# Second weights of experts 6 to 29 in one transfer each, in a one-core decoder layer with 32 experts

## The reference, cut to what matters

```python
hn = rms_norm(x, norm_ffn_g)
logits = hn @ router_w + router_b            # 256 x 32; the best 4 per token, softmax over them
gu = xb @ w_gu[e] + b_gu[e]                  # w_gu[e]: 1024 x 2048, float32, 8 MB
x_glu = minimum(gu[:, :1024], 7.0)
x_lin = clip(gu[:, 1024:], -7.0, 7.0)
act = x_glu * sigmoid(1.702 * x_glu) * (x_lin + 1.0)
y = act @ w_down[e] + b_down[e]              # w_down[e]: 1024 x 1024, float32, 4 MB
x = x + sum over the 4 experts of gate * y
out = rms_norm(x, norm_final_g)
```

## Time and profile before

| | before |
|---|---|
| runs of the kernel, median (lowest to highest) | 1183.41 us (1183.18 to 1184.78), 3 runs |
| the profiled execution, its own time | 1185.09 us |
| span of that execution in the trace | 1183.3 us |
| busy share of PE / DVE / ACT / POOL | 95% / 29% / 18% / 1% |
| data moved, mean rate over the span | 449.67 MB, 380 GB/s |
| mean granted clock of PE | 0.994 of full |

### The profile page before, as it was taken

How to read it: one execution, slowest core, us unless ns; L and a number is a source line. 1 busy time by engine, 2 the same in 40 slices (tenths; PEclk the granted TensorE clock), 3 DMA queues, 4 the chain that set the end, 5 groups by cost and what they waited for, 6 DMA issues and landing times.

```text
span 1183.3 us, 16067 instructions
## 1 busy us (share of the span) xinstructions
PE 1123.7 (95%) x6921; PEld 549.1 (46%) x6921; DVE 348.5 (29%) x668; ACT 217.9 (18%) x351; POOL 8.6 (1%) x20
## 2 busy tenths in 40 slices
PE   8999999999999999999999999999998999999996
PEld 8999878884333333333333333333333333333332
DVE  6747985556111111111111111111111211111112
ACT  5557666443000000000000000000000000000002
POOL 1000000001000000000000000000000000000000
PEclk9999999999999999999999999999999999999999
DMA  9645655799999999999999999999999999999995
GB/s 271 263 165 168 216 216 206 269 385 377 412 428 430 432 425 430 430 429 431 431 429 430 431 431 430 430 431 431 431 430 429 417 431 431 430 430 431 429 428 222
DMA packets 47993, 449.67 MB, mean 380 GB/s; under 512 B 6352, under 2 KB 9488, under 8 KB 30224
## 3 DMA queue, kind: packets, MB, share of 16 engines
q1 hardware_dynamic: 47392, 447.70, 90.8%
q10 hardware_dynamic: 560, 1.36, 0.5%
HBM read 447.48 MB, written 1.05 MB: 379 GB/s over the span
## 4 chain that ended last, share of the span: by engine, by line
PE 52%; DMA 42%; DVE 4%; ACT 2%; issue 1%; SPq 0%; ACTq 0%; DVEq 0%
DMA dn<-in_w_down 32%; PE ps L790 16%; PE ps L824 13%; DMA gu<-in_w_gu 7%; PE ps L520 6%; PE ps L526 3%; DMA dn_last<-in_w_down 2%; PE ps L499 2%; PE ps L503 2%; PE ps L500 2%; PE ps L767 2%; PE ps L730 2%; PE ps L708 1%; PE ps L808 1%; DVE w_lo L1245 0%
## 5 line engine op out<-in xcount | busy, mean ns | idle before, releaser
L790 PE MATMUL ps<-gu,xg 128*64 128x512 f32 x2048 | 450.8, 598 | 6.3 <-DMA gu<-in_w_gu 6.3
L790 PEld LDWEIGHTS ps<-gu,xg 128*64 128x64 f32 x2048 | 144.7, 138 | 308.7 <-issue 297.6
L824 PE MATMUL ps<-dn,actT 128*64 128x512 f32 x992 | 223.2, 597 | 36.7 <-DMA dn<-in_w_down 36.5
L1567 DVE TENSOR_SCALAR g<-ps 128x512 f32<-128x512 f32 x32 | 22.1, 692 | 660.4 <-PE ps L790 660.4
L824 PEld LDWEIGHTS ps<-dn,actT 128*64 128x64 f32 x992 | 67.1, 137 | 183.3 <-issue 116.0
L767 PE MATMUL ps<-y_sb,wT 64*128 64x512 f32 x248 | 67.6, 633 | 0.0
L1142 ACT ACTIVATE wT<-ps 128x256 f32<-128x256 f32 x22 | 8.5, 384 | 313.1 <-PE ps L802 313.1
L499 PE MATMUL ps<-x_hi,w_hi 128*128 128x256 f32 x256 | 65.0, 290 | 1.1 <-DVE x_lo L1252 1.1
L500 PE MATMUL ps<-x_lo,w_hi 128*128 128x256 f32 x256 | 63.6, 285 | 0.0
L1245 DVE TENSOR_TENSOR w_lo_rows<-land,w_hi_rows 128x1024 fp32r<-128x1024 f32 x48 | 56.5, 1218 | 19.7 <-ACT w_hi_rows L967 19.6
L1148 ACT ACTIVATE y_sb<-ps 128x512 f32<-128x512 f32 x22 | 13.1, 597 | 265.0 <-PE ps L824 265.0
(11 more groups left out here) (259 smaller groups left out, 875.8 us busy)
## 6 DMA issues: line engine op xcount, KB each, us to landing
gu<-in_w_gu SPq DMA_DIRECT2D x54, 4096.0 KB, 27.1
dn<-in_w_down SPq DMA_DIRECT2D x62, 2048.0 KB, 23.4
gu<-in_w_gu SPq DMA_DIRECT2D x20, 2048.0 KB, 13.1
land<-in_w_in SPq DMA_DIRECT2D x13, 2048.0 KB, 8.0
land<-in_w_proj_rnn SPq DMA_DIRECT2D x2, 2048.0 KB, 7.7
land<-in_w_proj_attn SPq DMA_DIRECT2D x2, 2048.0 KB, 9.3
land<-in_w_out SPq DMA_DIRECT2D x2, 2048.0 KB, 7.8
dn_last<-in_w_down SPq DMA_DIRECT2D x1, 2048.0 KB, 27.0
```

The source lines that it names most:

```text
L790: last = mm(ps[64 * h:64 * h + 64, 4 + c, :], xg[:, k * SLOTS:(k + 1) * SLOTS], gu[par][m // 2][:, m % 2 * 2 + r, c * D + h * HALF:c * D + ...
L824: last = mm(ps[64 * h:64 * h + 64, bank, :], src[:, j, half * SLOTS:(half + 1) * SLOTS], room[:, j, h * HALF:(h + 1) * HALF], start=half = ...
```

## The change

D(6) to D(29) are each loaded by one transfer of 4 MB into `dn_whole`, which lies where `dn[0]` and `dn[1]` lie; partition p holds eight adjacent rows (32 KB) instead of four rows of each half (16 KB each). SP waits for both halves of down(e-1) before it issues D(e), where it waited for each half. PE waits once, for the whole D(e), before down(e) (`down_whole`), with the same 32 products as before; it still raises `dn_used` twice. So that the activations match the new order of rows, DVE reads the PSUM bank with a step of eight columns instead of four, and `turn_act` makes 16 products of 64 x 64 outputs with one half of the identity each in the place of the four transposes. Experts 0 to 5, 30 and 31 keep two halves, and so do the further passes (taken only when an expert has more than 64 tokens, line 255).

```diff
+DN_WHOLE = 8
...
+        dn_whole = at("dn_whole", 64, [P, DN_WHOLE, D])
...
-        def by_rows(t):
-            return t.rearrange("q (j p) -> q j p", j=DN_RUN)
-
-        def by_columns(t):
-            return t.rearrange("q (p j) -> q j p", j=DN_RUN)
+        def by_rows(t, run=DN_RUN):
+            return t.rearrange("q (j p) -> q j p", j=run)
+
+        def by_columns(t, run=DN_RUN):
+            return t.rearrange("q (p j) -> q j p", j=run)
...
+            def load_whole(row, used):
+
+                sp.wait_ge(dn_used, used)
+                sp.dma_start(dn_whole[:, :, :], w_dn_rows[ds(row, D), :].rearrange("(p j) n -> p j n", p=P)).then_inc(
+                    whole_landed, 16)
...
             load_gu(RING * D + D, 1, lambda m: sp.wait_ge(gu_used, 4 * RING + (m + 1 - 4)))
-            load_dn(RING * D, lambda h: sp.wait_ge(dn_used, 2 * RING + (h + 1 - 2)))
+            load_whole(RING * D, 2 * RING)
             with sp.Fori(RING // 2 + 1, N_E // 2 - 1, 1) as i:
                 load_gu(i * (2 * D), 0, lambda m: sp.wait_ge(gu_used, 4 * (2 * i) + (m + 1 - 8)))
-                load_dn(i * (2 * D) - D, lambda h: sp.wait_ge(dn_used, 4 * i + (h + 1 - 4)))
+                load_whole(i * (2 * D) - D, 4 * i - 2)
                 load_gu(i * (2 * D) + D, 1, lambda m: sp.wait_ge(gu_used, 4 * (2 * i) + (m + 1 - 4)))
-                load_dn(i * (2 * D), lambda h: sp.wait_ge(dn_used, 4 * i + (h + 1 - 2)))
+                load_whole(i * (2 * D), 4 * i)
             E = N_E - 2
             load_gu(E * D, 0, lambda m: sp.wait_ge(gu_used, 4 * E + (m + 1 - 8)))
-            load_dn((E - 1) * D, lambda h: sp.wait_ge(dn_used, 2 * E + (h + 1 - 4)))
+            load_whole((E - 1) * D, 2 * E - 2)
             for m in range(4):
                 sp.wait_ge(gu_used, 4 * E + (m + 1 - 4))
...
+            def turn_act(E, par, whole=False):
                 pe.wait_ge(act_ready, E + (par + 1))
+                if whole:
+                    for j in range(DN_WHOLE):
+                        for h in range(2):
+                            rows = slice(64 * h, 64 * h + 64)
+                            last = mm(ps[rows, 7, j * SLOTS:(j + 1) * SLOTS], act_s[:, j * SLOTS:(j + 1) * SLOTS],
+                                      ident[:, rows], start=True, stop=True)
+                    last.then_inc(actT_filled, 1)
+                    return
                 for j in range(4):
                     last = nc.tensor.transpose(ps[:, 7, j * P:(j + 1) * P], act_s[:, j * P:(j + 1) * P], ident[:, :])
                 last.then_inc(actT_filled, 1)
...
-                pe.wait_ge(dn_landed[half], 16 * e + 16 * (5 - RING))
+
+                pe.wait_ge(dn_landed[half], 16 * e - 16 * (N_E - 2 - 5))
...
+            def down_whole(e, bank=6):
+
+                pe.wait_ge(whole_landed, 16 * e - 16 * (RING - 1))
+                for j in range(DN_WHOLE):
+                    for h in range(2):
+                        last = mm(ps[64 * h:64 * h + 64, bank, :], actT[:, j // 2, j % 2 * SLOTS:(j % 2 + 1) * SLOTS],
+                                  dn_whole[:, j, h * HALF:(h + 1) * HALF], start=j == 0, stop=j == DN_WHOLE - 1)
+                    if j % DN_RUN == DN_RUN - 1:
+                        last.then_inc(dn_used, 1)
...
-                turn_act(E, par)
+                turn_act(E, par, second is None)
...
-                for half in range(2):
-
-                    room = second(E + (par - at_once), half)
-                    down(half, room).then_inc(dn_used, 1)
+                if second:
+                    for half in range(2):
+
+                        room = second(E + (par - at_once), half)
+                        down(half, room).then_inc(dn_used, 1)
+                else:
+                    down_whole(E + par)
...
                 if not first:
-                    for half in range(2):
-                        down(half, wait_second(E + (par - 1), half)).then_inc(dn_used, 1)
+                    down_whole(E + (par - 1))
...
-                turn_act(E, par)
+                turn_act(E, par, whole)
...
-            step(N_E - 2, 0)
+            step(N_E - 2, 0, whole=False)
...
-                        expert(p * N_E + 2 * i, p * PER_PASS + 2 * i - 1, par, at_once=True)
+                        expert(p * N_E + 2 * i, p * PER_PASS + 2 * i - 1, par, at_once=True, second=wait_second)
...
-                V.tensor_scalar(by_rows(g1[:, :]), by_columns(ps[:, 4, :]), LIMIT, None, ALU.min).then_inc(glu_ready, 1)
-                V.tensor_scalar(by_rows(l1[:, :]), by_columns(ps[:, 5, :]), LIMIT, -LIMIT, ALU.min, ALU.max).then_inc(gu_read, 1)
+                V.tensor_scalar(by_rows(g1[:, :], run), by_columns(ps[:, 4, :], run), LIMIT, None, ALU.min).then_inc(glu_ready, 1)
+                V.tensor_scalar(by_rows(l1[:, :], run), by_columns(ps[:, 5, :], run), LIMIT, -LIMIT, ALU.min, ALU.max).then_inc(gu_read, 1)
...
-            with dve.Fori(1, STEPS // 2, 1) as i:
+            with dve.Fori(1, RING // 2, 1) as i:
                 for par in range(2):
                     expert(2 * i, 2 * i, 2 * i, par)
+            with dve.Fori(RING // 2, STEPS // 2, 1) as i:
+                for par in range(2):
+                    expert(2 * i, 2 * i, 2 * i, par, run=DN_WHOLE)
             with dve.Fori(STEPS // 2, N_E // 2 - 1, 1) as i:
                 for par in range(2):
-                    expert(2 * i, 2 * i, 2 * i, par, 7)
+                    expert(2 * i, 2 * i, 2 * i, par, 7, DN_WHOLE)
```

More of the change, by code:

```diff
@@ L200, in program @@
         early_landed = [[sem(f"early_landed{p}_{m}") for m in range(4)] for p in range(2)]
-        dn_landed = [sem(f"dn_landed{r}") for r in range(3)]
+        dn_landed, whole_landed = [sem(f"dn_landed{r}") for r in range(3)], sem("whole_landed")
         (vec_landed, rope_landed, wx_landed, wa_landed, b4_landed, rw_landed, rbb_landed,
@@ L803, in turn_weights @@
                 last.then_inc(wT_filled, 1)
-            def turn_act(E, par):
+            def turn_act(E, par, whole=False):
                 pe.wait_ge(act_ready, E + (par + 1))
+                if whole:
[6 more added lines that the diff above has]
+                    return
                 for j in range(4):
@@ L827, in down, with expert @@
                 return last
-            def expert(E, X, par, meanwhile=None, first=False, at_once=False, early=0, second=wait_second):
+            def down_whole(e, bank=6):
[6 more added lines that the diff above has]
+                        last.then_inc(dn_used, 1)
+            def expert(E, X, par, meanwhile=None, first=False, at_once=False, early=0, second=None):
                 up(E, X, par, first, early, at_once)
@@ L860, in expert, with step @@
                     combine(par, 1)
-            def step(E, par, first=False):
+            def step(E, par, first=False, whole=True):
                 pe.wait_ge(wT_ready, E + par)
@@ L1563, in _, with activation @@
             dve.wait_ge(parts_ready, TT)
-            def activation(E, par):
+            def activation(E, par, run=DN_RUN):
                 dve.wait_ge(gu_used, 4 * E + 4 * (par + 1))
-                V.tensor_scalar(by_rows(g1[:, :]), by_columns(ps[:, 4, :]), LIMIT, None, ALU.min).then_inc(glu_ready, 1)
-                V.tensor_scalar(by_rows(l1[:, :]), by_columns(ps[:, 5, :]), LIMIT, -LIMIT, ALU.min, ALU.max).then_inc(gu_read, 1)
+                V.tensor_scalar(by_rows(g1[:, :], run), by_columns(ps[:, 4, :], run), LIMIT, None, ALU.min).then_inc(glu_ready, 1)
+                V.tensor_scalar(by_rows(l1[:, :], run), by_columns(ps[:, 5, :], run), LIMIT, -LIMIT, ALU.min, ALU.max).then_inc(gu_read, 1)
                 dve.wait_ge(gu_read, E + (par + 2))
@@ L1578, in keep_actT, with expert @@
                 V.tensor_copy(to[:, :, :], ps[:, 7, :].rearrange("p (j s) -> p j s", j=4)).then_inc(actT_ready, 1)
-            def expert(E, X, e, par, bank=6):
+            def expert(E, X, e, par, bank=6, run=DN_RUN):
                 build(e + (par + 1), 1 - par)
-                activation(E, par)
+                activation(E, par, run)
                 dve.wait_ge(gathered, X + (par + 2))
```

## The result

| | before | changed |
|---|---|---|
| runs of the kernel, median (lowest to highest) | 1183.42 us (1183.18 to 1184.78), 5 runs | 1190.72 us (1188.29 to 1191.22), 5 runs |
| ratio, 95% interval | | 1.0048 (1.0037 to 1.006) |
| profiled execution, its own time / span | 1185.09 / 1183.3 us | 1190.79 / 1189.1 us |

The change costs about 0.5%, some 5.7 us, in the direction and at the place that were forecast, and 1.6 us more than the 4.1 of the sum. The ratio of 1.0048 gives 1189.1 on the 1183.41 from which the sum started. The medians alone lie 7.3 us apart, and the median itself, 1190.72, lies just above the range; with five runs that scatter over 2.9 us I go by the ratio.

What follows compares the result with a forecast made beforehand. The transfer stream bounds the kernel, fed with nothing in hand where the order changes. A hole at D(23) costs 4.6 us, larger pieces return 0.5; 4.1 added to 1183.41 gives 1187.5 us, range 1185.0 to 1190.3.

Steps and rivals of the forecast that it cites:

- the sum: Whole kernel: stream 4.6 us late at D(23), 0.5 given back by six more experts; 4.1 added to 1183.41.
- What bounds the kernel: Whole kernel: the transfer stream bounds; the queue has nothing in hand only where the order changes, at expert 22.
- The pieces: Loads of D: 32 KB pieces instead of 16 KB save 0.08 us per expert, bounds 0 and 0.16.
- Rival C: Loads of D: one 4 MB transfer is cheaper than G's rows say; at 0.5 us per expert 1178.3; chance 0.06.
- The one wait in form `expert`: Before down(e): two 1.2 us waits become one of about 2.4, PE work 3.44 us later; no price there.
- The turn: Sixteen products replacing four transposes: price by columns 0, taken as 0.25 us, hidden in the wait in form `expert`.
- DVE's step of eight: DVE reading PSUM with step eight instead of four: taken as 0, far bound 1.4 us.
- The sum to D(23): From D(21)'s landing: down(21) starts 893.9, D(23) is issued 945.8 and lands 958.4 on an idle queue.
- rival A: At down(21): the clock falls in the merged wait, D(23) issued 1.7 us later, 1189.2 us; chance 0.16.
- rival B: At D(23)'s issue: hole covered if PE is 6.3 us earlier than in the sum; 1181.6 us; chance 0.10.

Runs made afterwards that it cites:

- e4: Kernel before with one wait moved: D(23)'s first half waits for both halves of down(22); 1187.36 us, ratio 1.0022 to the kernel before.
- e3: Changed kernel, still one transfer and one wait, but old row order (16 KB runs), four transposes, DVE step of four; 1192.9 us, ratio 1.0076.
- e7: Changed kernel, loops cut open, D(20) and D(21) in two transfers with two waits each, D(22) and D(23) whole; 1185.1 us, ratio 1.001.
- e6: Changed kernel, loops cut open, with the turn by four transposes again for all experts; 1189.3 us, ratio 1.0054 to the kernel before.
- the control: Changed kernel with its loops over the experts cut open at experts 20 to 25, nothing else changed; 1189.63 us, ratio 1.0051.
- e2: Changed kernel with D(6) to D(29) in two transfers and two waits on each side again; new rows, turn, DVE step kept; 1184.79 us, ratio 1.0007.
- e8: Changed kernel with D(20) to D(23) exactly as in the kernel before, the other twenty whole; 1183.64 us, ratio 0.9998.
- e9: The kernel of e8 measured once more to narrow its interval; 1183.98 us, ratio 0.9996 to the kernel before.
- e1: Changed kernel with eight more bf16 products on PE in each wait for D(e) of experts 6 to 21; 1188.54 us, ratio 1.0042.

## Why the prediction was right, point by point

- **What bounds the kernel.** Right: the stream of transfers, fed with nothing in hand only where form `expert` gives way to `step`. The one hole is there and nowhere else, and e4 shows that an issue 3.6 us later there is 2.6 us of time by the ratio, 3.5 by the medians.
- **The pieces.** Right, 0.08 us per expert: a period of 29.13 us against 29.21 in e3 and 29.22 before. Rival C (one transfer costs less than the rows of G say) fell with it, and with it the fixed cost of about 2 us that the Trainium skill names ("DMA: Bandwidth & Descriptors", section on the anatomy of one DMA) as a gain to be had here. That section is about transfers issued by GpSimd's software path, and the transfers of this kernel ran on a hardware queue (q1 hardware_dynamic on the page of the profile), which the prediction did not say.
- **The one wait in form `expert`.** Right that it has no price there and makes the issue of D(23) 3.44 us later where the order changes (e7). The wait is 2.09 to 2.51 us at nine of the fifteen downs and not at all of them; at the other six, each right behind a slow down, it is 0.39 to 1.20.
- **The turn.** The step that failed by size: 0.25 us were taken, 0.5 is right (0.55 by the rows, 1.15 against 0.60, and 0.49 in e6). The cause is a misreading of rows 10. The row with four plain products of 512 columns holds two calls; every float32 product stands in the trace as two instructions, a transpose as one, as the sixteen calls of the turn now appear as x32. The 64 and 32 products counted for `up` and `down` are such instructions, the 16 of the turn are calls. A plain float32 product with 512 columns therefore takes 0.88 us, 1.7 ns a column, and a transpose 0.8: the transpose mode is twice as fast by this case's rows. By that, an estimate, the 8 x 64 columns of the turn cost 0.88 us instead of 0.41, about the 0.5 that was measured; the price by columns, put at 0, was the error. The Trainium skill ("TensorE: Matmul & The Clock Gate", table of terms) says four times: its direction was right and was wrongly put aside, its size is not what the rows show.
- **DVE's step of eight.** Right at 0: from up(22) to the turn it is 921.15 - 903.75 = 17.40 us in the changed kernel and 17.40 (917.16 - 899.76) before.
- **The sum to D(23).** Forecast 945.8 for the issue without a fall, 51.9 us after down(21) starts; the control had 944.83 with a start 1.0 earlier than forecast, so 51.97, the changed kernel 947.83 with the fall, 53.81. The landing of 4 MB on an idle queue, forecast at 12.6, took 12.4.
- **The fall of the clock, rival A.** Its price (1.7) and its rule (a fall takes from the next wait, so only the one at down(21) counts) were right, its chance was not. I gave it 0.16 with the argument that not each wait need have it. The rule itself says more: if a long wait brings a fall and a fall makes the next wait short, about every other down has one, and 7 of 15 had. The chance should have been near one half; then the likeliest time lies about 1 us higher and the range with it. The 5.7 us are, as an account and not as a measured split, the 4.1 of the sum, 0.3 for the turn and, in part of the executions, 1.7. The forecast of 1187.5 was 1.6 us low; that 1189.1 lies in the range is owed to its upper end, which came from this rival.
- **The other side, rival B.** It needed PE 6.3 us earlier, and only giving up both parts of the wait, as e2 (first half issued at 938.77) and e8 (937.98) do, brings that.

## What to carry to other kernels

Look for the one place where a full queue is fed with nothing in hand, here where the order of the work changes, and price every wait by what it adds up to there, not by the many places where it is free. Halves at that place alone brought the time back to that of the kernel before (e8, e9); a gain from the large transfers elsewhere was not shown. Merging two waits into one cost twice here: the work behind it starts later by half its length (3.44 us), and the longer dead time can cost the clock (1.7 us). Before a row of counts is turned into a price, check how many instructions of the trace one call makes.

## What the runs showed of the hardware

Among the fifteen waits for D(7) to D(21) in the changed kernel's trace, nine left PE idle for 2.09 to 2.51 us, and seven of these nine were followed by the lower level of the clock (0.50 of full from 895 to 898 us, after 2.09 us idle); the other six waits, of 0.39 to 1.20 us, each behind a down at the lower level, were not. With eight bf16 products in the wait and at most 0.98 us of idle left none was (e1). The period of an expert, 12 MB, was 0.08 us shorter with D in runs of 32 KB than in runs of 16 KB, with one transfer each (29.13 us in the changed kernel against 29.21 in e3). A transfer of 4 MB issued to an empty queue landed after 12.4 us, 2.7 more than the 9.7 that it takes of a full one.
